# First mixer's recurrence in blocks of 128 tokens, both directions' scores in one tile, second decay on GpSimd

## What is computed

```python
def gla_chunked(q, k, v, g, s0):            # GLA_CHUNK = 64
    b = jnp.cumsum(gc, axis=2)              # within a chunk of 64
    b_last = b[:, :, -1:]
    q_dec = qc * jnp.exp(b)
    k_intra = kc * jnp.exp(-b)
    k_state = kc * jnp.exp(b_last - b)
    scores = jnp.where(mask, jnp.einsum('bnthd,bnshd->bnhts', q_dec, k_intra), 0.0)
    o_intra = jnp.einsum('bnhts,bnshv->bnthv', scores, vc)
    def step(S, xs):
        qd, ks, vv, bl = xs
        o = jnp.einsum('bthd,bhdv->bthv', qd, S)
        S = S * jnp.exp(bl)[..., None] + jnp.einsum('bthd,bthv->bhdv', ks, vv)
        return S, o
    ...
    return o_intra + o_inter, s_final

def gla_bidirectional(q, k, v, g_fwd, g_bwd, s_fwd0, s_bwd0):
    o_f, s_f = gla_chunked(q, k, v, g_fwd, s_fwd0)
    o_b, s_b = gla_chunked(flip(q), flip(k), flip(v), flip(g_bwd), s_bwd0)
    return o_f + flip(o_b), s_f, s_b
```

## Time and profile before

| | us |
|---|---|
| device time, median of 3 runs (1333.8 to 1337.12) | 1335.58 |
| span of the profiled execution, first to last instruction | 1332.1 |
| median less that span (launch and end around it) | 3.5 |
| TensorE busy in it | 1305.4 (98%) |
| stretch from the first modulation unit of the recurrence to the transposes after it (137.3 to 214.9) | 77.6 |
| VectorE / ScalarE / GpSimd busy in that stretch | 58.4 / 33.0 / 6.3 |

### The profile page before, as it was taken

How to read it: one execution, slowest core, us unless ns; L and a number is a source line. 1 busy time by engine, 2 the same in 40 slices (tenths; PEclk the granted TensorE clock), 3 DMA queues, 4 the chain that set the end, 5 groups by cost and what they waited for, 6 DMA issues and landing times.

```text
span 1332.1 us, 22086 instructions
## 1 busy us (share of the span) xinstructions
PE 1305.4 (98%) x8104; PEld 1089.2 (82%) x8104; DVE 573.3 (43%) x1093; ACT 685.5 (51%) x1096; POOL 707.6 (53%) x307
## 2 busy tenths in 40 slices
PE   5999999999999999999999999999999999999999
PEld 1688567787888888888777757999999987999999
DVE  3423683225544344301146365455532485456620
ACT  4561345334544444422247745666665667766652
POOL 1432004352544444445336212688899775888897
PEclk8999999999999999999999999999999999999999
DMA  9532634471322332443544252665566541565564
GB/s 364 185 95 95 260 134 161 147 279 48 126 94 94 96 101 99 155 166 110 162 153 138 79 206 80 216 192 199 192 202 211 174 143 48 196 197 192 191 206 125
DMA packets 60132, 210.16 MB, mean 158 GB/s; under 512 B 6432, under 2 KB 9760, under 8 KB 59936
## 3 DMA queue, kind: packets, MB, share of 16 engines
q1 hardware_dynamic: 59632, 207.52, 45.9%
q10 hardware_dynamic: 432, 1.70, 0.3%
HBM read 208.15 MB, written 1.05 MB: 157 GB/s over the span
## 4 chain that ended last, share of the span: by engine, by line
PE 93%; DVE 3%; ACT 1%; DMA 1%; SPq 1%; issue 1%; ACTq 0%; DVEq 0%
PE ps L352 74%; PE ps L479 2%; PE ps L407 1%; PE ps L1117 1%; PE ps L389 1%; PE ps L399 1%; PE ps L1501 1%; DMA raw<-wstream 1%; PE ps L1132 1%; PE ps L1480 1%; PE ps L1124 1%; SPq L314 1%; PE ps L1111 1%; PE ps L1483 1%; PE ps L498 1%
## 5 line engine op out<-in xcount | busy, mean ns | idle before, releaser
L341 POOL TENSOR_TENSOR wlo<-raw,whi 128x1024 fp32r<-128x1024 f32 x291 | 695.3, 2406 | 609.2 <-ACT whi L336 608.7
L336 ACT ACTIVATE whi<-raw 128x1024 fp32r<-128x1024 f32 x291 | 306.5, 1056 | 213.2 <-PE ps L352 148.1
L352 PE MATMUL ps<-Hhi_,whi 128*128 128x256 f32 (+1 forms) x1336 | 388.5, 319 | 0.0
L352 PE MATMUL ps<-Hlo_,whi 128*128 128x256 f32 (+1 forms) x1336 | 385.0, 316 | 0.0
L352 PEld LDWEIGHTS ps<-Hhi_,whi 128*128 128x128 f32 x1336 | 251.0, 188 | 22.2 <-issue 4.1
L352 PEld LDWEIGHTS ps<-Hlo_,whi 128*128 128x128 f32 x1336 | 251.0, 188 | 19.4 <-issue 1.4
L352 PE MATMUL ps<-Hhi_,wlo 128*128 128x256 f32 (+1 forms) x1336 | 231.8, 316 | 0.0
L352 PEld LDWEIGHTS ps<-Hhi_,wlo 128*128 128x128 f32 x1336 | 194.5, 188 | 18.1
L352 PE MATMUL ps<-hidhi,whi 128*128 128x256 f32 (+1 forms) x528 | 151.1, 315 | 0.0
L352 PE MATMUL ps<-hidlo,whi 128*128 128x256 f32 (+1 forms) x528 | 150.7, 314 | 0.0
L775 ACT ACTIVATE u<-ps,par 128x256 f32<-128x256 f32 (+1 forms) x132 | 83.9, 635 | 114.7 <-PE ps L352 101.3
(11 more groups left out here) (334 smaller groups left out, 1575.2 us busy)
## 6 DMA issues: line engine op xcount, KB each, us to landing
raw<-wstream SPq DMA_DIRECT2D x367, 512.0 KB, 3.5
Haside_lo<-wstream SPq DMA_DIRECT2D x8, 512.0 KB, 5.7
Haside_hi<-wstream SPq DMA_DIRECT2D x8, 512.0 KB, 9.2
Paside<-wstream SPq DMA_DIRECT2D x4, 512.0 KB, 4.9
XT<-x_t SPq DMA_DIRECT2D x1, 1024.0 KB, 10.0
XT<-ctx_t SPq DMA_DIRECT2D x1, 1024.0 KB, 12.2
memx<-mem_t ACTq DMA_DIRECT2D x1, 1024.0 KB, 5.8
out_t<-XT SPq DMA_DIRECT2D x1, 640.0 KB, 6.1
```

What stands on the lines that cost most here:

```text
L336: nc.scalar.activation(whi[:, n % RING, :], raw[:, r % RAWS, :], ACT.Copy).then_inc(S["hi_ready"], 1)
L341: nc.gpsimd.tensor_tensor(wlo[:, r, :], raw[:, r, :], whi[:, n % RING, :].bitcast(F32), ALU.subtract).then_inc(S["lo_ready"], 1)
L352: mm = nc.tensor.matmul(o, a, b, start=start, stop=stop)
```

## The change

States are passed between blocks of 128 tokens, not chunks of 64. The decays are still taken within chunks of 64, so a block has one half whose queries need the other half's whole decay too, and one half whose keys for the state do. GpSimd multiplies these in place (`gla_pool`, new; `decayed` on half of `kstf` and on half of `qdec`, `gdec` the product of the two totals of a block), signal `g_decay`. That happens after the round's scores, which need them without. Within a block, queries of one half now also meet keys of the other half: four more matmuls of 64x64 outputs from `kstf` and `qdec`. Both directions' scores go into one tile `am`, one triangle each. On the diagonal both directions have the same value, so GpSimd doubles it once per head (`twice`, ones plus the identity), and the backward mask leaves it out. VectorE makes three states a round in place of seven. Output within blocks is then made once per head.

The order is new as well. TensorE starts a round with its scores and takes the outputs from the states of the round before after them; VectorE prepares products one round ahead and sums two; ScalarE makes exponentials two rounds ahead. GpSimd's loop over the weight slots is cut at `gr`, and `gla_pool` stands there.

```diff
-        ORDER = [[0, 1, 2, 3, 4, 5, 6, 7], [3, 2, 1, 0, 7, 6, 5, 4]]
+        ORDER = [[0, 1, 2, 3], [1, 0, 3, 2]]
+        SC_BANK = (5, 3)
...
+            def score(c):
+                b, bank = c % 2, SC_BANK[c % 2]
+                pe.wait_ge(S["g_q"], 3 * c + 3)
+                if c >= 2:
+                    pe.wait_ge(S["g_am"], c - 1)
+                for tt in range(NB):
+                    sl = slice(tt * P, (tt + 1) * P)
+                    nc.tensor.matmul(ps[:, bank, sl], kint[:, b, sl], qdec[:, b, sl], start=True, stop=True)
+                for tt in range(NB):
+                    halves = [slice(tt * P + i * CH, tt * P + (i + 1) * CH) for i in range(2)]
+                    key, query = halves if b == 0 else halves[::-1]
+                    mm = nc.tensor.matmul(ps[CH * b:CH * b + CH, bank, query], kstf[:, b, key], qdec[:, b, query], start=True, stop=True)
+                mm.then_inc(S["g_sc"], 1)
+            def state_turns(c):
+                pe.wait_ge(S["g_decay"], keys_decayed(c))
...
+            def updates(c):
...
+                for j in range(NB - 1):
+                    tt = ORDER[d][j]
+                    mm = nc.tensor.matmul(update(j), kst[:, tt, :], gv[:, tt, h * 256:(h + 1) * 256], start=True, stop=True)
...
+            def between_blocks(c):
+                if d == 0 and h >= 1:
+                    pe.wait_ge(S["g_of"], h)
+                pe.wait_ge(S["g_decay"], queries_decayed(c))
+                for j in range(1, NB):
+                    tt = ORDER[d][j]
+                    pe.wait_ge(S["g_S"], (NB - 1) * c + j)
+                    mm = nc.tensor.matmul(out_rows(tt), qdec[:, c % 2, tt * P:(tt + 1) * P], Sh[:, j, :],
...
             for c in range(2 * GH):
                 h, d = divmod(c, 2)
+                score(c)
                 if c >= 1:
+                    between_blocks(c - 1)
+                state_turns(c)
+                if d == 0:
+                    mod_products(pe, 0, {0: 5, 2: 7, 4: 8, 6: 10}[c])
+                else:
+                    within_blocks(h)
+                updates(c)
+                if c == 3:
                     mod_turn(pe, 2)
+                elif d == 1:
+                    mod_products(pe, 0, {1: 6, 5: 9, 7: 11}[c])
+            between_blocks(2 * GH - 1)
+            mod_turn(pe, 3)
...
+            exps(1)
             for c in range(2 * GH):
...
                 after(c)
                 if c % 2 == 0 and c >= 2:
+                    stats(c // 2 - 1)
                     scaled(c // 2 - 1)
+                if c + 2 < 2 * GH:
+                    exps(c + 2)
+            hi_slot(act, START["gr"])
+            hi_slot(act, START["gr"] + 1)
+            mod_row(act, 3)
+            stats(GH - 1)
             scaled(GH - 1)
+            hi_slot(act, START["gr"] + 2)
+            hi_slot(act, START["gr"] + 3)
...
+            masked(0)
+            for c in range(1, 2 * GH):
+                states(c - 1)
+                if c == 4:
+                    mod_bias(dve, 2)
+                masked(c)
                 if c + 1 < 2 * GH:
                     second(c + 1)
+                if c + 2 < 2 * GH:
+                    first(c + 2)
+            states(2 * GH - 1)
...
+            for c in range(2 * GH):
+                d = c % 2
+                pool.wait_ge(S["g_e"], 4 * c + 4)
+                pool.wait_ge(S["g_sc"], c + 1)
+                decayed(kstf, c, d)
+                tot = gtot[:, c % 2, :].rearrange("p (b a) -> p a b", a=2)
+                nc.gpsimd.tensor_tensor(gdec[:, c % 2, :], tot[:, 0, :], tot[:, 1, :], ALU.mult)
+                decayed(qdec, c, 1 - d)
+                if d == 0:
+                    pool.wait_ge(S["g_am"], c + 1)
+                    x = am[:, :].rearrange("p (a t) -> p a t", t=P)
+                    nc.gpsimd.tensor_tensor(x, x, twice[:, :].rearrange("p (a t) -> p a t", a=1).to_broadcast([P, NB, P]), ALU.mult).then_inc(S["g_decay"], 1)
```

More of the change, by code:

```diff
@@ L34 @@
 NCH = TT // CH
+NB = TT // P
 GH, MH, AH, MEMH = 4, 8, 8, 4
@@ new lines, in state_turns @@
+            def state_turns(c):
+                pe.wait_ge(S["g_decay"], keys_decayed(c))
+                for tt in range(NB):
+                    mm = nc.tensor.transpose(ps[:, 0, tt * P:(tt + 1) * P], kstf[:, c % 2, tt * P:(tt + 1) * P], ident)
+                mm.then_inc(S["g_kt"], 1)
+            def updates(c):
+                h, d = divmod(c, 2)
+                pe.wait_ge(S["g_kst"], c + 1)
+                for j in range(NB - 1):
+                    tt = ORDER[d][j]
+                    mm = nc.tensor.matmul(update(j), kst[:, tt, :], gv[:, tt, h * 256:(h + 1) * 256], start=True, stop=True)
+                mm.then_inc(S["g_U"], 1)
@@ L1094, in gla_pe, with within_blocks @@
+            def within_blocks(h):
+                pe.wait_ge(S["g_am"], 2 * h + 2)
+                for tt in range(NB):
+                    nc.tensor.matmul(out_rows(tt), am[:, tt * P:(tt + 1) * P], gv[:, tt, h * 256:(h + 1) * 256],
+                                     start=False, stop=False, skip_group_check=True)
             for c in range(2 * GH):
                 h, d = divmod(c, 2)
-                if c in (0, 2):
-                    mod_products(pe, 0, 5 + c)
-                b = c % 2
@@ L1100, in gla_pe @@
-                pe.wait_ge(S["g_q"], 3 * c + 1)
+                score(c)
                 if c >= 1:
[L1102 to L1133, removed]
@@ L1332, in gla_dve @@
                     first(1)
-            for c in range(2 * GH):
-                if 1 <= c and c + 1 < 2 * GH:
-                    first(c + 1)
-                third(c)
+                    second(1)
+                    first(2)
+            masked(0)
[4 more added lines that the diff above has]
+                masked(c)
                 if c + 1 < 2 * GH:
                     second(c + 1)
-                if c == 2 or c == 7:
-                    mod_bias(dve, 2 if c == 2 else 3)
+                if c + 2 < 2 * GH:
+                    first(c + 2)
+            states(2 * GH - 1)
+            mod_bias(dve, 3)
             gain_scale(dve, 0, 1, 4)
@@ L2356, in _ @@
             so = START["so"]
-            run(0, so)
+            run(0, START["gr"])
+            gla_pool(pool)
+            run(START["gr"], so)
             even_pair(pool, 0)
```

80 lines of the change are left out of this document (45 added, 35 removed).

## The result

| | before | after |
|---|---|---|
| device time, median (4 runs each, side by side) | 1334.69 us (1333.5 to 1337.12) | 1319.75 us (1319.02 to 1320.54) |
| ratio, 95% interval | | 0.9887, 0.9873 to 0.9901 |
| profiled execution: its time, its span | 1333.8, 1332.1 | 1320.3, 1318.1 |
| stretch, from the end of the wait for the value copies to the output transposes | 77.57 | 62.10 |

A forecast was written before the change was run, and what follows sets the result against it. TensorE was taken as the bound, VectorE right behind. 19.2 us removed, less 6.8 for cross scores and 0.75 for a first wait, gave 11.65 off: span 1320.4, plus 3.5 around it, 1323.9 us; range 1320.5 to 1329.5.

The forecast's parts named there:

- The bound: TensorE, busy 1305.4 of 1332.1 us, bounds the kernel; in the recurrence VectorE is right behind.
- Full-width groups at 0.24 per instruction: TensorE's 256-column instructions at 0.24 us: six make 1.44 for updates or outputs from states, eight make 1.92 within blocks.
- a rival: Dear scores on TensorE: 64x64 matmuls at 1.06 plus array-division changes, 3.7 us more, 1327.6; chance 0.08.
- Cross scores at 0.85: Four added 64x64 score matmuls a round on TensorE at 0.85 us, between 0.53 and 1.06: 6.8 us in eight rounds.
- the upper row: Price from above for the 64x64 scores: the 128x128 scores with 128 columns, 1.06 us a group.
- Transposes, `mod_turn`s, units: TensorE's other recurrence work, with no saving forecast; transposes priced at 0.49 us, a modulation unit at 1.86.
- Waits: TensorE's `kint` waits, 1.3 us, go; 0.7 for value copies stays; one 0.75 wait for GpSimd comes in round 0.
- Cover: Other hand-overs in the recurrence hide behind TensorE's work, forward rounds' states by 0.4 us at the worst, ScalarE by about 1.
- GpSimd against VectorE: Two-SBUF-input VectorE and GpSimd instructions exclude each other; 1.6 us delay of forward sums, no TensorE wait; masks and states clear.
- The sum: 19.2 - 6.8 - 0.75 = 11.65 us off the recurrence: stretch 65.9, span 1320.4, with 3.5 around it 1323.9 us.
- The range: 1320.5 to 1329.5 us: cross scores at their lower bound without the first wait, up to over the two larger rivals.

The follow-up runs named there:

- two tiles: Changed kernel with separate masked scores and outputs within blocks for each direction again, diagonal not doubled: 1326.19 us, ratio 0.9943, stretch 68.63.
- interleaved kernels: Changed kernel with each cross product right behind its 128x128 score: 1327.56 us, stretch 69.80; the same with whole weight loads, array undivided: 1320.21 us, stretch 63.07.
- whole-load kernel: Changed kernel with cross scores made with all 128 keys as weights and 64 queries, array undivided: 1321.07 us, ratio 0.9886, stretch 63.07.
- doubled load: Changed kernel with GpSimd's half-block products and diagonal doubling done twice, extras into a spare tile: 1325.14 us, ratio 0.9942, stretch 67.55.

## Why the prediction was wrong in its size

**The bound**: right. TensorE stayed at 98%, and what was taken from it came off the end.

Two steps failed, both prices: the 0.24 us for a full-width instruction and the 0.85 us for a group of cross scores.

**Full-width groups at 0.24 per instruction**: the term that failed most widely. The 0.24 was read from L1124, which stood between L1117 and L1132, both on a divided array, so its 1.92 held the price of changes. Between undivided neighbours it is 1.73 (two tiles), 0.216 each. This entered three terms: the four groups of outputs within blocks that stay (0.8 too dear), the updates (0.5) and the outputs from states (0.2; the forecast of 1.44 a group became 1.38 and 1.42 in the mean), 1.4 us in all. Another 0.3 us came from the old outputs from states, which took 18.1 us where 2.34 and 1.87 a group give 17.8. The prediction saw 0.25 us for two changes in L1117, and even counted that four changes a round become two, but used it only to judge a rival and credited nothing. The interleaved kernels put 0.11 to 0.16 us on a change in the middle of a group of scores, the whole-load kernel and the one without cross scores 0.05 to 0.10 on one at a group's edge, so there is not one price. No run changed the neighbours of L1124 in the kernel before itself; that its 0.19 was such a price is inferred from these kernels. The Trainium skill (TensorEngine Tiling (Array Packing), Key Properties) says that switching the mode drains TensorE. The runs agree that a switch costs time (0.05 to 0.16 us), not why, and this speaks for the change, which has fewer switches, while the prediction took the rule as a rival against it.

**Cross scores at 0.85**: mis-sized by 1.6 us. They took 0.61 in rounds without a wait, 5.17 over the eight (0.65 each). It is near the bound from half the weights (0.53), and far from the upper row to which the prediction thought it nearer. The bound itself was a slip: the 1.06 of L498 is its duration, and from start to start it took 0.91, which halves to 0.46. The loaded weights count for more than the columns: with whole loads and the same 64 columns the group takes 0.84, with whole loads and 128 columns 0.89. Counted with what they do to their neighbours the cross scores cost 0.81 in an undisturbed round, but the prediction's other prices, 1.06 and 1.44, already had room for that.

**Transposes, `mod_turn`s, units**: forecast unchanged, and 0.7 us cheaper; the transposes (0.54 to 0.49) and turns (0.91 to 0.81) lost a divided neighbour.

**Waits**: right. One wait for GpSimd in round 0, 0.82 for 0.75; both for `kint` gone; the value copies at 0.72 stay. GpSimd's half product took 0.62, forecast 0.57, and its doubling 1.28, forecast 1.04.

**Cover**: nearly right, and partly by luck. In rounds 2 and 4 VectorE's first state came 0.1 us too late in place of 0.4 to 0.6 early, which cost 0.4 us (two tiles). In round 2, counted from the end of its scores (156.06), it was ready after 6.7, forecast 6.6, but two errors hide in that: VectorE's 0.76 us wait for `g_o` was left out, and GpSimd's part was put at 1.6 where it cost 1.0, since its product of the queries (157.00 to 157.62) fell into that idle time. What used up the cover is that TensorE got there at 6.8 and not at 7.2. Taking the cross scores out of each round or doubling GpSimd's work brings the wait at once. The work of VectorE in a round adds up, from the prediction's own terms, to 7.9 to 8.6 us and not 8.2 to 8.7; nothing hangs on it.

**GpSimd against VectorE**: right in kind, as the 1.67 us product, and the 2.28 us scan under doubled load, show; the rule of the Trainium skill (SBUF — State Buffer, Who interferes with whom) agrees, also in that the masks, with one input in PSUM, kept 0.74 beside GpSimd's products. What the prediction did not ask is whether VectorE could do this work itself: it can, at 0.6 us.

**The sum**: the stretch was forecast at 65.9 and is 62.1. Four smaller differences nearly cancel. What lies around the span was taken as 3.5 us, the median of all runs less the span of one; the executions' own times put it at 1.7 before and 2.2 after, 1.3 us too much. The recurrence began 2.2 us later in the profile of after, 2.0 of it by the first weights. 1323.9 - 3.8 - 1.3 + 2.2 - 0.7 (after the recurrence) - 0.6 (the profiled execution above the median) = 1319.7.

**The range** ended at 1320.5 because its lower end moved only the cross scores to their bound and dropped the first wait; neither happened. The price of full-width instructions had no bound of its own, and it was the one that entered three terms.

## What to carry to other kernels

A group's time from start to start includes what its neighbours do to it: read the price of a shape between neighbours like those that it will have, and give a price that enters several terms its own bounds. Keep matmuls that divide the array together: eight changes a round in place of two cost 7.7 us here, half of what the change gains. When work per round shrinks, put independent work between a hand-over and its use: 12.6 of the 15 us depended on where the outputs from the states stand. And when an engine works a round ahead, look for what still reads the buffer that it will write: that wait, 0.76 us of VectorE, stood in no estimate.

## What the runs showed of the hardware

A change between whole and divided array cost 0.11 to 0.16 us in the middle of the scores and 0.05 to 0.10 at a group's edge. A 64x64 float32 score matmul (two instructions) took 0.15 us, one with whole weights and 64 columns 0.21, one with 128 columns 0.22 where no divided group stood next to it (L1121 without cross scores, 0.89 for four). For 256 elements in runs of 64 GpSimd took 0.62 us and VectorE 0.42; for 512 with a repeated operand 1.28 and 0.69, where the earlier trace rows had 1.04 for GpSimd. Meeting instructions of the two stretched both: 0.68 to 1.75, 1.22 to 2.28, and on GpSimd 0.62 to 1.06 and 1.28 to 1.71. And float32r matmuls of one shape ran 4% slower in one execution than in another (852 against 885 in 100 us), at the same granted clock.
